# Reordering the last attention step of a two-layer decoder trunk on one core

## The reference

```python
proj = h @ w_in                                  # 1024 -> 4 * 1536
q, k, v, z = jnp.split(proj, 4, axis=-1)
q = rope(rmsnorm(q.reshape(B, L, 12, 128), q_norm_w), pos)      # k likewise
for g, (window, dil) in enumerate(B_GROUPS):
    o, lse = dilated_window_attn(qg, k_all, v_all, start, k_start, dil, window // dil + 1)
lam = jax.nn.softmax(jnp.stack(lses, axis=0), axis=0)
o = jnp.concatenate([outs[g] * lam[g][..., None] for g in range(3)], axis=2)
y = (o * jax.nn.silu(z)) @ w_out                 # 1536 -> 1024
x = x + gate * y
```

## Time and profile before

| what | value |
|---|---|
| median of 3 runs | 1298.25 us (1298.18 to 1298.26) |
| the profiled execution | 1295.26 us |
| its span, first to last instruction | 1293.5 us |
| PE busy | 1218.8 us (94%) |
| DVE, ACT, POOL busy | 637.5, 499.6, 252.8 us |
| mean granted TensorE clock | 0.975 |

### The profile page before, as it was taken

How to read it: one execution, slowest core, us unless ns; L and a number is a source line. 1 busy time by engine, 2 the same in 40 slices (tenths; PEclk the granted TensorE clock), 3 DMA queues, 4 the chain that set the end, 5 groups by cost and what they waited for, 6 DMA issues and landing times.

```text
span 1293.5 us, 23446 instructions
## 1 busy us (share of the span) xinstructions
PE 1218.8 (94%) x9804; PEld 1127.4 (87%) x9804; DVE 637.5 (49%) x1045; ACT 499.6 (39%) x1004; POOL 252.8 (20%) x279
## 2 busy tenths in 40 slices
PE   6889999999999999976999899999999999997898
PEld 4689899989898989865999798999999899985898
DVE  3644656565656565565342653452454246333432
ACT  3642343434343434342121542553454254333321
POOL 1040314040404040400000160052034005200000
PEclk9989999999999999988999899999999999997999
DMA  9852425242434343311622426421742552151332
GB/s 263 274 159 66 146 87 147 86 145 89 135 98 132 102 131 102 115 53 46 201 66 82 151 83 155 120 78 43 174 111 61 128 148 69 52 135 50 127 107 62
DMA packets 242987, 148.11 MB, mean 115 GB/s; under 512 B 19385, under 2 KB 237241, under 8 KB 242370
## 3 DMA queue, kind: packets, MB, share of 16 engines
q1 hardware_dynamic: 228546, 134.81, 36.9%
q10 hardware_dynamic: 14336, 11.80, 2.8%
HBM read 124.56 MB, written 22.02 MB: 113 GB/s over the span
## 4 chain that ended last, share of the span: by engine, by line
PE 74%; issue 11%; DVE 5%; ACT 3%; SPq 3%; DMA 2%; POOL 2%; DVEq 0%; POOLq 0%; ACTq 0%
PE PJ L360 20%; PE PJ L1375 17%; PE PJ L1116 13%; PE PJ L374 3%; PE X L1563 1%; PE X L1094 1%; PE X L1028 1%; PE X L1489 1%; PE X L988 1%; PE X L1467 1%; PE X L1021 1%; PE PJ L1400 1%; PE X L1456 1%; PE PJ L388 1%; DVE dd L834 1%
## 5 line engine op out<-in xcount | busy, mean ns | idle before, releaser
L333 DVE TENSOR_TENSOR w_lo<-raw,w_hi 128x1024 fp32r<-128x1024 f32 (+1 forms) x128 | 156.5, 1237 | 204.9 <-ACT w_hi L325 204.3
L325 ACT ACTIVATE w_hi<-raw 128x1024 fp32r<-128x1024 f32 (+1 forms) x128 | 129.0, 1024 | 198.9 <-PE PJ L1375 98.2
L1375 PE MATMUL PJ<-w_hi,h_hi 128*128 128x256 f32 x600 | 172.3, 287 | 0.8 <-issue 0.8
L1375 PE MATMUL PJ<-w_lo,h_hi 128*128 128x256 f32 x600 | 169.7, 283 | 0.0
L1375 PE MATMUL PJ<-w_hi,h_lo 128*128 128x256 f32 x600 | 169.7, 283 | 0.0
L360 PE MATMUL PJ<-h_hi,w_hi 128*128 128x288 f32 x736 | 163.5, 304 | 4.0 <-ACT v_ L772 4.0
L360 PE MATMUL PJ<-h_hi,w_lo 128*128 128x288 f32 x736 | 158.4, 297 | 0.0
L360 PE MATMUL PJ<-h_lo,w_hi 128*128 128x288 f32 x736 | 158.3, 297 | 0.0
L360 PEld LDWEIGHTS PJ<-h_hi,w_hi 128*128 128x128 f32 x736 | 119.0, 190 | 10.0 <-issue 9.9
L360 PEld LDWEIGHTS PJ<-h_hi,w_lo 128*128 128x128 f32 x736 | 119.3, 190 | 0.0
L360 PEld LDWEIGHTS PJ<-h_lo,w_hi 128*128 128x128 f32 x736 | 119.3, 190 | 0.0
(11 more groups left out here) (295 smaller groups left out, 2416.5 us busy)
## 6 DMA issues: line engine op xcount, KB each, us to landing
raw<-in_a_w_in_dram SPq DMA_DIRECT2D x48, 512.0 KB, 3.9
raw<-in_ada_w_dram SPq DMA_DIRECT2D x32, 512.0 KB, 3.8
raw<-in_b_w_in_dram SPq DMA_DIRECT2D x64, 256.0 KB, 3.4
kvc<-in_cache_kv_w_dram SPq DMA_DIRECT2D x24, 512.0 KB, 5.6
pre<-in_ada_w_dram SPq DMA_DIRECT2D x16, 512.0 KB, 8.6
s<-in_state_hgrn_dram SPq DMA_DIRECT2D x8, 1024.0 KB, 6.6
out_hgrn_sample_dram<-s ACTq DMA_DIRECT2D x8, 1024.0 KB, 5.1
raw<-in_a_w_out_dram SPq DMA_DIRECT2D x16, 512.0 KB, 4.9
```

The source lines that it names most:

```text
L325: act.activation(w_hi[:, i % SPLITS, 0:size], raw[:, n % RAWS, 0:size], ACT.Copy).then_inc(hi_done, 1)
L333: dve.tensor_tensor(w_lo[:, i % SPLITS, 0:size], raw[:, n % RAWS, 0:size], w_hi[:, i % SPLITS, 0:size].bitcast(F32), ALU.subtract).then_in ...
L1375: last = pe.matmul(PJ[:, tile // 2, tile % 2 * 256:tile % 2 * 256 + 256], h_all[x][:, c0:c0 + P], b[:, k, :], start=(first and k == 0 and ...
```

## The change

Only the work from slot 8 of step 3 to output column 0 gets another order; its instructions stay the same ones. The loops over slots stop at 8 for step 3, step 4 is dropped, and the order is written out: `pe_last` for PE, and two blocks `if j == GH - 1` for ACT and DVE. `project_T` can do part of its eight k blocks, and the two last gate projections (slots 10 and 11) are each done as two halves. The operations of `act_attention` and `dve_attention` become small functions with unchanged bodies. The copies and subtractions of `oz` (`o1_hi`, `o1_lo`) move into the step; each of their blocks n now waits only for the gating of its own heads.

```diff
-        def project_T(t, key, cut=HT):
+        def project_T(t, key, ks=range(KD), cut=HT):
 
             nc.tensor.wait_ge(raw_split, split_no[key][0] + 1)
-            s = begin(t)
+            s = begin(t) if 0 in ks else t % 2
             wh, wl = parts_of(key)
-            for k in range(KD):
+            for k in ks:
...
-            last.then_inc(pj_ready, 1)
+            if KD - 1 in ks:
+                last.then_inc(pj_ready, 1)
...
+        def pe_last(pe):
+
+            j = GH - 1
+            tickets = {k: (ticket_a(j, k), ("a", j, k)) for k in range(8, 12)}
+            project_T(*tickets[8])
+            pe_st(pe, j, 0)
+            pe_s0(pe, j)
+            pe.wait_ge(ss_mask, 3 * j + 1)
+            project_T(*tickets[9])
+            pe_v0_rows(pe, j)
+            pe_s12(pe, j)
+            pe_kt(pe, j, 1)
+            project_T(*tickets[10], range(0, 4))
+            pe_st(pe, j, 1)
+            pe_kt(pe, j, 2)
+            project_T(*tickets[10], range(4, KD))
+            pe_st(pe, j, 2)
+            pe_kt(pe, j, 3)
+            project_T(*tickets[11], range(0, 4))
+            pe_st(pe, j, 3)
+            pe_pt0(pe, j, 0)
+            project_T(*tickets[11], range(4, KD))
+            pe_pt0(pe, j, 1)
+            pe_pts(pe, j, GH)
+            pe_pt12(pe, j, GH)
+            pe_m(pe, j, 0)
+            pe_ms(pe, j, GH)
+            pe_m(pe, j, 1)
+            pe_turn(pe, j)
+            pe_m(pe, j, 2)
...
+            def o1_hi(n0, n1):
+                for n in range(n0, n1):
+                    act.wait_ge(pj_ready, OUT1)
+                    act.wait_ge(o_read, n + 1)
+                    act.wait_ge(os1_read, n // 3 + 1)
+                    act.activation(o_hi(n), oz[:, n % 3 * GH + n // 3, :], ACT.Copy).then_inc(oh_done, 1)
...
+            if j == GH - 1:
+                split_hi(("a", j, 11))
+                vt0_out()
+                nc.scalar.preload_act_table_set("sigmoid_and_others")
+                z_sigmoid(9)
+                v0_out()
+                split_hi(("out1", 0, 0))
+                kt(1)
+                logs_and_exps()
+                exps(0)
+                exps(1)
+                kt(2)
+                exps(2)
+                weights_exp()
+                split_hi(("out1", 0, 1))
+                kt(3)
+                exps_s(j, 0)
+                exps_s(j, 1)
+                pt_out(j, 0, 0)
+                exps_s(j, 2)
+                seq_weights_exp(j)
+                z_sigmoid(10)
+                z_sigmoid(11)
+                pt_out(j, 1, 2)
+                split_hi(("out1", 1, 0))
+                pts_out(j)
+                o1_hi(0, 5)
+                pt_out(j, 2, 0)
+                o1_hi(5, 7)
+                rows_out(j)
+                o1_hi(7, BH)
...
+            if j == GH - 1:
+                split_lo(("a", j, 11))
+                mask_s(j, 0)
+                mask(0)
+                mask(1)
+                mask(2)
+                weigh(P, nm, wx, mn, s_max, 3 * j + 3, c_in)
+                z_gate(9)
+                split_lo(("out1", 0, 0))
+                mask_s(j, 1)
+                scale_p()
+                split_lo(("out1", 0, 1))
+                mask_s(j, 2)
+                seq_weigh(j)
+                seq_scale(j)
+                z_gate(10)
+                z_gate(11)
+                split_lo(("out1", 1, 0))
+                o1_lo(0, 2)
+                gate_o(j, 0)
+                o1_lo(2, 5)
+                gate_o(j, 1)
+                gate_seqs(j)
+                o1_lo(5, 6)
+                gate_o(j, 2)
+                o1_lo(6, BH)
...
-            for n in range(BH):
-                if n < 9:
-                    act.wait_ge(o_read, 9)
-                    act.wait_ge(os1_read, GH - 1)
-                    act.wait_ge(pj_ready, OUT1)
-                else:
-                    act.wait_ge(o_read, 12)
-                    act.wait_ge(os1_read, GH)
-                act.activation(o_hi(n), oz[:, n % 3 * GH + n // 3, :], ACT.Copy).then_inc(oh_done, 1)
...
-            for j in range(GH + 1):
+            for j in range(GH):
                 pe_attention(pe, j)
+            pe_last(pe)
```

## The result

The changed kernel takes 1280.7 us in the median (1280.07 to 1282.99, 4 runs) against 1298.22 us, a ratio of 0.987 with a 95% interval of 0.9853 to 0.9887. That is 17.5 us less; 16.6 were forecast. Measured again beside it, the kernel before had a median of 1296.55 us and the changed one 1279.95, so 16.6 us less: the difference itself scatters by about 1 us.

What follows compares the result with a forecast made beforehand. Before column 0 no engine is full: TensorE loses idle time and clock to waits. Column start moves from 1206.65 to 1190.0, 16.6 us less; 1298.25 - 16.6 = 1281.6 us, range 1278.7 to 1286.0.

Steps and rivals of the forecast that it cites:

- What bounded the kernel: TensorE nearly throughout; in the 31.35 us drain before column 0 no engine is full, costing idle time and half clock.
- ACT's order as the cause: In the drain, exponentials of groups 1 and 2 queue behind sigmoids of slots 10 and 11: 15.8 us delay.
- PE's work and the waits: From 1158.19, 30.8 us of PE work at clock 1.00; with queues side by side, column 0 starts at 1190.0.
- The one wait: Before `pe_pt12`, PE idles 0.9 us until ACT, after a table load and two sigmoids, copies the second `pt` half.
- The reserves: Spare times at PE's hand-overs in the new order, 0.1 to 0.5 us, expected to hold.
- The 0.5 us before `pe_st` 2: ACT's key copy is done at 1166.1 and wanted by `pe_st` 2 at 1166.6, 0.5 us to spare.
- Rival (b): Hand-overs before column 0 have too little spare time, giving waits of 2 to 5 us, 1283.6 to 1286.6; chance 0.12.
- The rival drawn from them: ACT stands still another load's length behind each table load, 2.1 us more, 1283.7; chance 0.05.
- The residual load: Issued about 0.6 us ahead of column 0, landing about 1.3 us before DVE needs it; nothing taken for it.
- The clock: Granted clock stays 1.00 from 1158 to the columns' end, since the longest idle time expected is 0.9 us.
- The slower rival: Half clock holds through the interleaved stretch; gain gone at 16.6 of 30.8 us, 1312 if all; chance 0.04.
- The distance to the median: Whole kernel: the median stays 3.0 us above the profiled execution, 1278.6 against 1281.6.

Runs made afterwards that it cites:

- run with PE kept busy: Kernel before, with 52 extra matmuls on TensorE in its last step whose results nobody reads; 1293.2 us, ratio 0.9977.
- kernel without a wait: Changed kernel, with projection 11's last k block behind `pe_pt0`'s second half and ACT's copy of that half ahead of slot 11's sigmoid; 1279.2 us, again 1278.8.
- kernel with whole projections: Changed kernel, with gate projections 10 and 11 whole and PE's pieces in the old order, ACT and DVE in the new; 1289.2 us, ratio 0.9941.
- kernel with late copies: Changed kernel, with all twelve copies and subtractions of `oz` behind the step's last operations on ACT and DVE; 1281.8 us, ratio 0.9889.

## Why the prediction was right

**What bounded the kernel.** Right, both halves of it. Idle time and clock together were the drain's cost; the run with PE kept busy puts 3.6 us on the clock and leaves 13.4 for the idle time.

**ACT's order as the cause.** Only partly. The prediction read 15.8 us of delay "by order alone" from ACT's queue. Moving those exponentials alone gave 2.7 us, 1.0 of it by the clock, since DVE's scaling stood behind the gates too and PE's projections stood ahead of the pieces that wait. With the new order on both ACT and DVE, but PE's old one, the stretch is 40.56 us; the halves on PE bring it to 31.51. That last step of 9.05 us is 4.8 us of waits (5.48 against 0.65); the rest, 4.2 us, is what the pieces took longer at the low clock. The halves on PE with the old order on ACT and DVE were not run, so what each queue's order is worth is known only for this sequence of steps.

**PE's work and the waits.** The list of pieces gave a column at 1190.0 from a `pe_kt` 1 at 1158.19, 31.8 us; measured are 31.5. The sum of PE's work alone was 30.8 us and the kernel without a wait takes 30.86. ACT's exponentials of group 1 start 5.2 us after `pe_kt` 1 ends (1165.30 in the profile after), where the list had 5.3. The one wait was forecast as 0.9 us and is 0.65, nearly all of the 0.3 us by which the list was too long. Its place was right and its reason was not: the prediction had ACT's table load and sigmoids delay the copy, which started at 1178.7 against a `pe_pt0` done at 1178.3. In the profile ACT gets free at 1180.33, just as the transposes are done, and the copy's own length sets the wait.

**The reserves.** The 0.5 us before `pe_st` 2 was tested by adding 2.57 us ahead of it: 2.06 came out. Rival (b) did not occur: PE's only wait is the one before `pe_pt12`, so every reserve held, though only this one was tested.

**The table loads.** The rival drawn from them is out. The Trainium skill, page ScalarE: Activation LUTs, section What ACT_TABLE_LOAD costs, gives 2.66 us for a switch with its drain. This case does not agree: here the loads stand 1.29 us apart, and with two more of them the stretch grew by 2.06 us, not by 4.8; the measurement decides.

**The residual load.** It was issued 0.5 us ahead of the column and landed 8.8 us later, 1.7 us before DVE wanted it, so the tail stayed 86.8 us.

**The clock.** That it would stay at 1.00 was right; what the prediction took as the proof was too little. It judged by the longest single idle time (4.76 us with a fall, 1.37 without). In the kernel with whole projections it fell after three idle times of 1.0 to 1.1 us, and in the kernel with late copies after one of 1.54 us behind small pieces. So the 0.9 us that the prediction expected did not by itself rule out a fall; that part of the forecast came out right on too thin a ground. The slower rival needed 16.6 us of full-clock work at half clock; the most that any run here lost to the clock in the stretch was about 4 us.

**The distance to the median.** This term was wrong twice, and the errors cancel in part. The prediction kept the 3.0 us between the profiled execution and the median. The profiled execution after was 1.6 us slower than the 1278.6 us forecast for it, as its front part, which the change doesn't touch, took 1.9 us more; and the median lay 0.5 us above it and not 3.0. So that 1281.6 lies within 0.9 us of 1280.7 is partly luck; what the argument forecast is the stretch. In the twelve profiles the end of `pe_kt` 1 lies between 1158.0 and 1163.2 us. The front part's scatter was not traced to a cause.

## What to carry to other kernels

Where a drain alternates between engines, write the in-order queues side by side, with the durations of the profile, and cut a large independent piece of the bounding engine so that a part lies behind every hand-over; that forecast the length of a 31.5 us stretch to 0.3 us. Reorder all queues of the chain together: ACT's order alone shortened the stretch by 2.7 of the 16.9 us. Compare a change of this size by one stretch of the profile, between two events that it can't move; the time of the whole kernel scatters by more than the smaller edits here are worth.

## What was not expected of the hardware

The length of the longest idle time does not tell whether the clock falls. It fell in the kernel with whole projections after three idle times of about 1.1 us between 1176.0 and 1181.6, with TensorE busy for 2.54 of the 4.70 us from 1175.3; it did not fall after 2.00 us between dense projections (two loads ahead of the exponentials), and the same 1.21 us before column 0 was followed by 1.00 in one kernel and by 0.60 in another. A fall can cost about as much again as the idle time before it: 2.8 us on top of a wait of 3.10, and 1.6 on top of one of 1.54.
